# Fourier channel transform cut to columns 0 to 128 of cosine and sine in a two-layer HGRN2 / Fourier / MoE step

## The reference, cut to what matters

```python
def _fourier_mixer(h, w_out):
    B, L, _ = h.shape
    hg = h.astype(jnp.float32).reshape(B, L, FOURIER_GROUPS, FOURIER_CG)      # 4 groups of 256 channels
    z = jnp.fft.fftn(hg, axes=(1, 3), norm='ortho').real.reshape(B, L, D_MODEL)
    return jnp.einsum('bld,de->ble', z.astype(h.dtype), w_out)
...
x = x + g1 * out
h = _modulate(_rmsnorm(x, ...), sh2, sc2)
x = x + g2 * _hier_moe(h, ...)
```

## Time and profile before

| | |
|---|---|
| median of three runs | 1154.33 us (1151.06 to 1156.53) |
| profiled execution, its own time | 1151.34 us |
| its span in the profile | 1149.5 us |
| TensorE busy | 961.3 us, 84% of the span |
| VectorE, ScalarE, GpSimd busy | 19%, 20%, 15% |
| mean DMA rate over the span | 276 GB/s |
| mean granted TensorE clock | 0.937 of full |

### The profile page before, as it was taken

One profiled execution on the slowest core, in us unless ns is written; L12 is line 12 of the kernel. 1 busy time (PEld: TensorE's weight loads), 2 busy tenths in 40 slices (PEclk: granted clock), 3 DMA queues, 4 the chain that ended last, 5 costly groups with the idle time before them and its releaser, 6 DMA issues.

```text
span 1149.5 us, 19105 instructions
## 1 busy us (share of the span) xinstructions
PE 961.3 (84%) x7675; PEld 532.9 (46%) x7676; DVE 220.4 (19%) x515; ACT 224.8 (20%) x407; POOL 170.8 (15%) x287
## 2 busy tenths in 40 slices
PE   3799899999889993999899997399947999978760
PEld 0455445754445652555455553255434555534330
DVE  1100334301334342010000000600340101000005
ACT  1111000321001231222122221420221222211112
POOL 2001002111000130212121221210111221211112
PEclk9899999999899996999999999599987999999995
DMA  9974354356342665699999993970354899999954
GB/s 381 320 286 178 148 193 151 132 209 253 140 150 76 258 237 235 259 421 421 422 418 418 422 385 106 407 315 1 127 209 168 332 368 421 422 422 420 419 244 164
DMA packets 68466, 317.79 MB, mean 276 GB/s; under 512 B 13252, under 2 KB 15588, under 8 KB 53184
## 3 DMA queue, kind: packets, MB, share of 16 engines
q1 hardware_dynamic: 54592, 290.68, 63.1%
q0 software_dynamic: 9856, 18.51, 4.5%
q10 hardware_dynamic: 3968, 7.87, 1.9%
HBM read 308.62 MB, written 17.38 MB: 284 GB/s over the span
## 4 chain that ended last, share of the span: by engine, by line
PE 39%; DMA 18%; DVE 5%; issue 2%; SPq 2%; ACT 2%; POOLq 0%; POOL 0%; DVEq 0%; ACTq 0%
PE ps L836 14%; DMA ring<-in_moe_w_down 9%; PE ps L843 9%; PE ps L732 7%; DMA deep<-in_moe_w_down 6%; PE ps L753 2%; SPq L366 2%; DMA deep<-hrow,gi 1%; PE ps L812 1%; PE ps L769 1%; PE ps L532 1%; DMA deep<-yrows 1%; DMA yrows<-deep,si 1%; DVE deep L1366 1%; PE ps L817 1%
## 5 line engine op out<-in xcount | busy, mean ns | idle before, releaser
L836 PE MATMUL ps<-ring,deep 128*64 128x256 f32 x1600 | 184.8, 389 | 13.0 <-DMA ring<-in_moe_w_up 9.6
L836 PEld LDWEIGHTS ps<-ring,deep 128*64 128x64 f32 x1600 | 120.7, 140 | 83.5 <-issue 17.8
L556 PE MATMUL ps<-deep,ring 128*128 128x384 f32 x384 | 129.5, 495 | 4.2 <-ACT deep L927 4.2
L1362 DVE TENSOR_TENSOR deep<-deep,ps 128x128 f32<-128x128 f32 x76 | 18.4, 284 | 452.2 <-PE ps L836 452.2
L556 PEld LDWEIGHTS ps<-deep,ring 128*128 128x128 f32 x384 | 72.9, 193 | 58.3 <-issue 10.3
L843 PE MATMUL ps<-ring,deep 128*64 128x512 f32 x400 | 93.0, 607 | 8.3 <-DVE deep L1366 8.3
L836 PE MATMUL ps<-deep 128*64 128x256 f32 x832 | 92.8, 380 | 5.1 <-DMA deep<-in_moe_w_up 4.7
L559 PE MATMUL ps<-ring,deep 128*128 128x512 f32 x192 | 95.5, 654 | 0.0
L732 PE MATMUL ps<-ring,deep 128*128 128x512 f32 x192 | 83.8, 594 | 1.4 <-ACT deep L990 0.8
L836 PEld LDWEIGHTS ps<-deep 128*64 128x64 f32 x832 | 60.9, 137 | 40.6 <-issue 6.2
L490 PE MATMUL ps<-ring,scond 128*32 128x512 f32 x384 | 53.0, 675 | 17.0 <-DMA ring<-in_w_mod 16.2
(11 more groups left out here) (161 smaller groups left out, 801.0 us busy)
## 6 DMA issues: line engine op xcount, KB each, us to landing
ring<-in_w_mod SPq DMA_DIRECT2D x24, 2048.0 KB, 12.1
ring<-in_moe_w_gate SPq DMA_DIRECT2D x22, 2048.0 KB, 22.8
ring<-in_moe_w_up SPq DMA_DIRECT2D x22, 2048.0 KB, 27.5
ring<-in_moe_w_down SPq DMA_DIRECT2D x22, 2048.0 KB, 32.6
ring<-in_hgrn_w_in SPq DMA_DIRECT2D x10, 2048.0 KB, 8.0
deep<-in_moe_w_gate SPq DMA_DIRECT2D x10, 2048.0 KB, 20.4
deep<-in_moe_w_up SPq DMA_DIRECT2D x10, 2048.0 KB, 25.0
deep<-in_moe_w_down SPq DMA_DIRECT2D x10, 2048.0 KB, 30.6
```

The costliest lines, as they stand in the source:

```text
L556: last = mm(bank[:, 0:T], W[:, k, b * P:(b + 1) * P], hT[:, k, :], start=(k == 0), stop=(k == KD - 1))
L836: last = mm(ps[g * SLOTS:(g + 1) * SLOTS, GU_BANK[j], 0:2 * P], xt[:, b, h * SLOTS:(h + 1) * SLOTS], slot3(S[j])[:, k, g * F // 2:(g + 1) ...
```

## The change

The channel transform is formed only for columns 0 to 128 of the cosine and of the sine matrix, so its moving operand has 2 x 129 = 258 columns in place of 512, and each copy to `U` has 258 columns too. The position transform makes the lower half of a group (channels 0 to 127) from columns 0 to 127, and an upper half from columns 1 to 128, with the sine matrix added in place of subtracted. That gives channels 255 down to 128, in reversed order; for this the rows of the output weights in each upper half are reversed before the kernel is built. The stationary pieces of `U` now start at columns 0, 1, 129 or 130 of a row of 258, where they started at multiples of 128. `dft_ctx` and `dft_lat` each get a third matrix (plus sine), so their loads grow from 128 KB and 512 KB to 192 KB and 768 KB, while that of `dft_c` shrinks from 512 KB to 258 KB.

```diff
-        U = fo.take(TT * 4 * C512).rearrange("p (t g n) -> p t g n", t=TT, g=4)
-        dft_c = fo.take(2 * C512).rearrange("p (k n) -> p k n", k=2)
-        dft_ctx = fo.take(2 * P).rearrange("p (c n) -> p c n", c=2)
-        dft_lat = fo.take(4 * 2 * P).rearrange("p (t c n) -> p t c n", t=2, c=2)
+        FOLD = P + 1
+        U = fo.take(TT * 4 * 2 * FOLD).rearrange("p (t g n) -> p t g n", t=TT, g=4)
+        dft_c = fo.take(2 * 2 * FOLD).rearrange("p (k n) -> p k n", k=2)
+        dft_ctx = fo.take(3 * P).rearrange("p (c n) -> p c n", c=3)
+        dft_lat = fo.take(2 * 3 * 2 * P).rearrange("p (t c n) -> p t c n", t=2, c=3)
...
-                            last = mm(ps[:, 4 + n % 4, :], hT[:, 2 * g + k, t * P:(t + 1) * P], dft_c[:, k, :],
+                            last = mm(ps[:, 4 + n % 4, 0:2 * FOLD], hT[:, 2 * g + k, t * P:(t + 1) * P], dft_c[:, k, :],
                                       start=(k == 0), stop=(k == 1))
...
-                    g, o = k // 2, (k % 2) * P
+                    g, high = k // 2, k % 2
                     bank = ps[:, k % 4, :]
                     for c in range(2):
-                        mm(bank[:, 0:P], U[:, 0, g, c * 256 + o:c * 256 + o + P], dft_ctx[:, c, :],
+                        o = c * FOLD + high
+                        mm(bank[:, 0:P], U[:, 0, g, o:o + P], dft_ctx[:, c * (1 + high), :],
                            start=(c == 0), stop=(c == 1))
                     for t in range(2):
                         for c in range(2):
-                            last = mm(bank[:, P:T], U[:, 1 + t, g, c * 256 + o:c * 256 + o + P], dft_lat[:, t, c, :],
+                            o = c * FOLD + high
+                            last = mm(bank[:, P:T], U[:, 1 + t, g, o:o + P], dft_lat[:, t, c * (1 + high), :],
                                       start=(t + c == 0), stop=(t + c == 2))
...
-                A(U[:, n // 4, n % 4, :], ps[:, 4 + n % 4, :], ACT.Copy).then_inc(u_evac4, 1)
+                A(U[:, n // 4, n % 4, :], ps[:, 4 + n % 4, 0:2 * FOLD], ACT.Copy).then_inc(u_evac4, 1)
...
-    dft_c = np.concatenate([cc, sc], 1).reshape(2, P, 512).transpose(1, 0, 2)
+    dft_c = np.concatenate([cc[:, 0:P + 1], sc[:, 0:P + 1]], 1).reshape(2, P, 2 * P + 2).transpose(1, 0, 2)
     c1, s1 = dft(P)
-    dft_ctx = np.stack([c1, -s1], 1)
-    dft_lat = np.stack([cc, -sc], 1).reshape(2, P, 2, 256).transpose(1, 0, 2, 3)
+    dft_ctx = np.stack([c1, -s1, s1], 1)
+    dft_lat = np.stack([cc, -sc, sc], 1).reshape(2, P, 3, 256).transpose(1, 0, 2, 3)
...
+    rows = arrays["fourier_w_out"].reshape(1, 4, 2, P, D)
+    arrays["fourier_w_out"] = _np.ascontiguousarray(
+        _np.stack([rows[:, :, 0], rows[:, :, 1, ::-1]], 2).reshape(1, D, D))
```

## The result

The changed kernel takes 1142.07 us (median of 7 runs, 1141.74 to 1149.8) against 1154.57 us for the kernel before (7 runs). The ratio is 0.991, 95% interval 0.9885 to 0.9938, so 7 to 13 us less. The forecast was 1143.0 us, faster.

A forecast was written before the change was run, and what follows sets the result against it. TensorE was taken to bound the Fourier transforms, with a DMA-bound end moving along. Savings of 10.1 us (channel transform) and 0.2 us (last copy) from 1153.3 us gave 1143.0 us, range 1138.5 to 1148.5 us.

The forecast's parts named there:

- The bound of the stage: Through both Fourier transforms the chain is TensorE almost alone, so time taken out of L753 leaves the path there.
- L753, 48 records at 0.211 us, 10.1 us: Channel transform: 258 columns cost 0.218 us a record instead of 0.429, saving 3.4 us a tile, 10.1 us over three.
- The first tile: First channel-transform tile: starts at the low clock for 3.8 us, falls from 8.8 to 5.4 us, saving 3.4 us.
- rival 1: Channel transform: clock stays low throughout, 1152 to 1155 us, chance 5%; milder form, rise 2.6 us later, costs 1.3 us.
- Does the load bind, and the uneven starts: Weight loads stay hidden behind 258-column records; uneven stationary starts in the position transform cost nothing, at most 1.6 us.
- Rivals 3 and 4: Uneven starts slow the position transform, up to 1179 us, 3%; channel-transform step does not scale with columns, 1148.2 us, 3%.
- The copies: ScalarE's copies to U: 258 columns take 385 ns; eleven of twelve are hidden, the last exposed one saves 0.21 us.
- The moved waits: Modulation and output weights, Fourier matrices, a VectorE copy and early expert loads still arrive in time; cost nothing.
- The end moves rigidly: Expert loads are released by work behind the Fourier transform, so the DMA-bound end comes earlier by the whole gain.
- rival 2: The DMA-bound end absorbs the gain, time about 1149 to 1153 us; chance of losing over half 7%.
- Rival 5: Expert passes: rounding moves a token over a 64-slot limit, one pass more or less, near 12 us; 1% each way.
- The number: Whole kernel: a saving of 10.3 us from a mean of 1153.3 us gives 1143.0 us.

The follow-up runs named there:

- e2: The changed kernel with the channel transform's moving operand back at 512 columns (254 filler columns), all else kept; ratio to the kernel before 0.9993.
- e12: The changed kernel with nine products without use on TensorE only ahead of each layer's first expert pass; ratio to the kernel before 0.9845.
- e4: The changed kernel with each 258-column product issued as two of 129, cosine and sine apart; ratio to the kernel before 0.9913.
- e3: The kernel before with every U piece moved by one element, so all 96 stationary pieces start off a 16-byte boundary; ratio to the kernel before 0.9999.
- e5: The changed kernel with no edit, profiled a second time; ratio to the kernel before 0.9894.
- e9: The changed kernel with no edit, profiled a third time; 1146.25 us in one run.
- e1: The kernel before with no edit, profiled a second time; ratio 0.9996.
- e10: The kernel before with no edit, profiled a third time; 1150.02 us in one run.
- e8: The changed kernel with eight unused products before the transposes of layer 1's first norm and nine before each layer's first expert pass; ratio to the kernel before 0.9894.
- e6: The kernel before with eight products without use on TensorE before the transposes of layer 1's first norm; ratio to the kernel before 1.0001.
- e7: The changed kernel with eight products without use on TensorE before the transposes of layer 1's first norm; ratio to the kernel before 0.9909.

## Why the prediction was right, step by step

**The bound of the stage.** Right. TensorE's records set the length of the stage and nothing took their place.

**L753, 48 records at 0.211 us, 10.1 us.** Right. Tiles two and three lost 3.38 us each, the forecast was 3.4; 384 columns gave 5.36 us (forecast 5.3). e2 shows that nothing else of the change carries the gain.

**The first tile.** The value of 5.4 us was right where the clock falls (e12: 5.41), and so was taking the low stretch as a time and not as a number of records: both widths lose the same, 8.80 - 7.11 = 1.69 us and 5.41 - 3.73 = 1.68 us. The Trainium skill (TensorE: Matmul & The Clock Gate, Part 1) says of warming up that it is a time and not a number of matmuls. The two losses agree with it. Two things were mis-read. The stage doesn't start at the low level; the clock is up at its first record and falls 0.5 us later, so the low stretch was 3.4 us long and not 3.8. That the sum still gave 5.4 us to the digit is luck: a stretch of 3.8 us costs 0.2 us too much, and 16 x 0.218 = 3.5 us for the tile at the full clock is 0.2 us under the 3.7 of the chain. And I kept the low stretch for the changed kernel "if the clock rises at the same moment", although that moment isn't the kernel's own: of the five profiles with 258 columns and nothing added right ahead of the stage (e4's split ones among them), four had no low stretch at all. That is the term mis-sized, 3.4 us forecast against 5.07 us in the two profiles compared. It should have stood in the sum's surroundings as 1.7 us up or down at this place. The milder form of rival 1 had only a loss there, 1.3 us; that the low stretch could be missing altogether, and gain 1.7 us, stood nowhere.

**Does the load bind, and the uneven starts.** Both at nothing, both right (e4, e3). Rivals 3 and 4 are refuted by the runs made for them. The estimate from the two spacings of the Trainium skill (TensorE: Matmul & The Clock Gate, Back-to-back issue gap) would have left 0.32 us a record. The measurement decides: 16 records of 258 columns take 3.7 us here, 0.23 us each with the start of the tile in it.

**The copies.** 387 ns against 385, 0.2 us exposed and saved. Right.

**The moved waits.** PE waited neither for modulation weights between the tiles nor for the output weights at 780.49. Right.

**The end moves rigidly.** Right up to the last load. From the load after the router to that after the first expert the changed kernel has 40.0 us, before 40.7, and the kernels with 512 columns alone spread over 38.9 to 40.7; from there to the last load all fourteen profiles have 179.4 to 179.8 us. The DMA-bound end took nothing back, so rival 2 has no room left. Behind the last load there is a step that the prediction didn't have: the last down product takes either 3.67 or 5.37 us. It took 5.37 in all three profiles of the changed kernel (after, e5, e9) and 3.67 in all three of the kernel before (before, e1, e10). From the first record of the channel transform to the end of the profile the three have 397.7 to 397.9 us, and the three of before 406.5 to 408.3: 8.7 to 10.6 us less, and not 12. Whether the change brings this step at the end with it, or three profiles fell that way, is open: e4 and e12, just as narrow, have 3.67 us.

**Rival 1** in its full form (a low clock through all tiles) never came. Its mild form, a different low stretch, is the real uncertainty of this stage, but in whole steps of 1.7 us.

**Rival 5.** It did not come: both profiles have, over the two layers, 2432 records of the gate-and-up products and 608 of the down products.

**The number.** 1154.57 x (1 - 0.9911) = 10.3 us from the ratio; with the second comparison of the same kernel (e5, 0.9894) it is between 10 and 12. The difference of the two medians, 12.5 us, is no better known than these ratios. The measurement doesn't tell whether the changed kernel meets the low stretch more rarely than the kernel before. That the forecast time, 1143.0 us, lies within 1 us of the measured 1142.07 is in part luck: its start of 1153.3 us was 1.3 us under the median of seven runs, and its gain 2.2 us under the difference of the medians.

**A faster version.** e12 stands at 0.9845 of before, 1140.29 us. The changed kernel had 0.9911 and 0.9894. The profile explains only part of this. The four transposes ahead of each first pass take 0.67 us in place of 1.13. The passes themselves, 8.66 and 8.59 us, lie inside the 8.4 to 10.1 us that the profiles without added products have there. e8 had both passes at 7.13 us and yet only 0.9894, with the products ahead of the channel transform costing it 1.7 us there and some 1.5 us on the way to the router. e12's interval lies below that of the changed kernel in the first comparison (0.9885 to 0.9938) and touches that of e5 (0.9868 to 0.9921) and of e8. So e12 is at least as fast as the changed kernel, why is open, and for e8 no gain over the changed kernel is shown.

## What to carry to other kernels

In a dense stretch take the step between records, scale it by the columns, and multiply: here this gave 10.3 us against a measured 10.4. Then ask of each later transfer what releases it; all releasers lay behind the edit here, and the gain arrived at the last load even in front of a DMA-bound end. Treat every place where TensorE resumes after an idle time as a term of its own (1.7 us here), look at the granted clock at several moments around it, and compare two kernels only at the same outcome of that term.

## What the runs showed of the hardware

The granted clock can rise during a burst of transposes, with TensorE idle for about 2 us after it, and fall when dense products have already begun. A difference of 0.3 us in the moment of the rise (-3.0 against -2.7 us) went with 1.7 us of the stage.

Products without use ahead of a stage don't always help. Ahead of the channel transform they raised the clock 9.1 us before it, shortened the transposes, and the clock fell in the tile nonetheless (e6: 8.80 us; e7 and e8: 5.41 us). Ahead of the first expert passes the same nine products gave 7.13 us in both layers in e8, and 8.66 and 8.59 us in e12. The traces show where the two differ, here in layer 1, e8 first and then e12 (PE's timeline, with the window 861.50 to 864.00 us of each):

```profile
848.62 10.19 PE L832 MATMUL ps<-const 128*128 128x512 f32 x18 [0.67 <-DVE slots_idx L1338]
860.11 0.66 PE L815 MATMUL ps<-const,deep 128*128 128x128 f32 x4 [1.30 <-DMA deep<-hrow,gi]
861.50:864.00 2.50, 2.46 (x24) 2.01 (x26) 0.00 (x0) 1.28 (x1) 1.40 (x3) 1.00 1.03 411
```

```profile
848.25 7.96 PE L832 MATMUL ps<-const 128*128 128x512 f32 x18 [0.68 <-DVE slots_idx L1335]
859.67 0.66 PE L815 MATMUL ps<-const,deep 128*128 128x128 f32 x4 [3.47 <-DMA deep<-hrow,gi]
861.50:864.00 2.50, 2.50 (x14) 1.59 (x12) 0.00 (x0) 1.14 (x1) 1.25 (x2) 0.50 1.03 413
```

In e12 the clock was up sooner, the added products were done 2.2 us sooner, TensorE then idled 3.47 us in place of 1.30, and the clock fell again at the start of the pass. Layer 0 shows the same with 2.87 against 0.57 us. A fixed number of added products thus covered the wait in one profile and not in the other.

The same step appears at the end. In the changed kernel the last pass's down product took the 5.37 us shown above, and in e4

```profile
1102.53 3.67 PE ps L848 x16
```

It is the same 16 records, 1.7 us apart, and the pauses of TensorE shortly ahead of them were nearly the same, 1.76 and 1.27 us in the changed kernel and 1.72 and 1.32 us in e4. So the length of the pauses alone doesn't decide it there.

The start of the Fourier stage moves by 6.6 us between two profiles of the unchanged kernel before (741.19 and 747.77 us in e1), and in e1 1.8 us less follow behind it; that is the 4.8 us by which their spans differ. Most of this difference between single runs thus arises ahead of the stage that was changed, and its cause was not looked into.
